# Splitting the last scaling and the residual add of an MoE block between VectorE and GpSimd

## The reference

```
y = routed + shared                     # 512 x 1024, the sum over the 8 experts of each token and the shared one
x = x + ga2 * rmsnorm(y, g_post_ffn)    # rmsnorm(y, g) = y * rsqrt(mean(y*y) + 1e-6) * g, mean over the 1024 channels
```

## Time and profile before

| | us |
|---|---|
| median of 3 runs | 1064.5 (1063.95 to 1066.36) |
| profiled execution, its own time | 1069.23 |
| its span in the trace | 1067.2 |
| granted TensorE clock, mean over the span | 0.981 |
| busy: TensorE / VectorE / ScalarE / GpSimd | 1020.3 / 872.1 / 645.2 / 295.4 |

### The profile page before, as it was taken

The page is one execution under the profiler, slowest core; times in us unless marked ns, Lnnn a source line. Parts: engine busy times, 40 slices in busy tenths (PEclk is TensorE's granted clock), DMA queues, the critical chain, the costliest instruction groups (busy, mean ns, idle before and its releaser), DMA issues.

```text
span 1067.2 us, 15239 instructions
## 1 busy us (share of the span) xinstructions
PE 1020.3 (96%) x4652; PEld 742.9 (70%) x4652; DVE 872.1 (82%) x1416; ACT 645.2 (60%) x743; POOL 295.4 (28%) x224
## 2 busy tenths in 40 slices
PE   4999999899998999999999999999999999999976
PEld 0687776567754777777777777777777777777732
DVE  1669877734768899999999889999989999999867
ACT  5334135733343678777777767777767777777511
POOL 1242231630302433223323213323313323332200
PEclk9899999989999999999999999999999999999997
DMA  9667752212254799999999999999999999999993
GB/s 338 263 223 280 267 179 97 69 30 90 99 217 146 284 376 373 364 381 379 393 386 381 360 367 359 377 376 385 369 364 345 364 343 328 353 354 362 361 413 152
DMA packets 71080, 318.67 MB, mean 299 GB/s; under 512 B 17232, under 2 KB 17744, under 8 KB 44560
## 3 DMA queue, kind: packets, MB, share of 16 engines
q1 hardware_dynamic: 36816, 200.30, 49.7%
q10 hardware_dynamic: 11616, 72.66, 17.9%
q0 software_dynamic: 22624, 45.40, 11.4%
HBM read 317.25 MB, written 39.85 MB: 335 GB/s over the span
## 4 chain that ended last, share of the span: by engine, by line
PE 80%; DVE 9%; DMA 7%; ACT 2%; issue 1%; ACTq 0%; SPq 0%; POOL 0%; DVEq 0%; POOLq 0%
PE ps L1348 11%; PE ps L1350 11%; PE ps L1349 11%; PE ps L1366 10%; PE ps L1033 8%; PE ps L1372 8%; PE ps L1123 6%; DMA hg<-h_rows,idxg 3%; PE ps L1225 2%; DMA yr<-y_rows 2%; PE ps L1285 2%; PE ps L1049 2%; PE ps L1305 1%; PE ps L1207 1%; DVE acc L1504 1%
## 5 line engine op out<-in xcount | busy, mean ns | idle before, releaser
L1821 DVE TENSOR_TENSOR wlo<-raw,whi 128x2048 fp32r<-128x2048 f32 x136 | 305.2, 2285 | 0.0
L891 ACT ACTIVATE whi<-raw 128x2048 fp32r<-128x2048 f32 x136 | 261.4, 1923 | 0.0
L1348 PE MATMUL ps<-whi,hthi 128*128 128x512 f32 x544 | 223.9, 412 | 0.0
L1350 PE MATMUL ps<-whi,htlo 128*128 128x512 f32 x544 | 213.5, 393 | 0.0
L1349 PE MATMUL ps<-wlo,hthi 128*128 128x512 f32 x544 | 212.7, 391 | 0.0
L661 POOL DMA_INDIRECT y_rows<-ysb,idxs x68 | 69.1, 1016 | 447.8 <-DVE idxg L1816 387.2
L934 ACT ACTIVATE ysb<-ps 128x1024 f32<-128x1024 f32 x68 | 69.8, 1026 | 176.1 <-PE ps L1372 176.1
L653 POOL DMA_INDIRECT hg<-h_rows,idxg x70 | 135.9, 1942 | 71.9 <-DVE idxg L1816 51.6
L1366 PE MATMUL ps<-rawd,actt 128*128 128x512 f32 x272 | 129.4, 598 | 1.9 <-ACT actt L927 1.9
L1350 PEld LDWEIGHTS ps<-whi,htlo 128*128 128x128 f32 x544 | 102.1, 188 | 22.3
L1349 PEld LDWEIGHTS ps<-wlo,hthi 128*128 128x128 f32 x544 | 102.6, 189 | 17.7
(11 more groups left out here) (273 smaller groups left out, 1608.7 us busy)
## 6 DMA issues: line engine op xcount, KB each, us to landing
raw<-in_w_gate_dram SPq DMA_DIRECT2D x68, 1024.0 KB
raw<-in_w_up_dram SPq DMA_DIRECT2D x68, 1024.0 KB
rawd<-in_w_down_dram ACTq DMA_DIRECT2D x66, 1024.0 KB, 10.1
ada<-in_w_ada_dram SPq DMA_DIRECT2D x24, 1024.0 KB, 7.8
yr<-y_rows SPq DMA_DIRECT2D x6, 2048.0 KB, 19.1
wraw<-in_w_in_dram POOLq DMA_DIRECT2D x8, 1024.0 KB, 5.6
woraw<-in_w_out_dram SPq DMA_DIRECT2D x16, 256.0 KB, 2.7
yr<-y_rows SPq DMA_DIRECT2D x8, 512.0 KB, 10.1
```

The lines of the kernel that those rows point to most:

```text
L891: A(whi[:, s, m_, :], raw[:, s, m_, :], ACT.Copy).then_inc(hi_ok, 1)
L1348: mm(out_, hthi[s][:, k, :], hi, start=(k == 0), stop=False)
L1350: ins = mm(out_, htlo[s][:, k, :], hi, start=False, stop=(k == KD - 1))
L1821: V.tensor_tensor(wlo[s][:, m_, :], raw[:, s, m_, :], whi[:, s, m_, :].bitcast(F32), ALU.subtract).then_inc(lo_dve, 1)
```

## The change

VectorE's `rows_done(t)` no longer calls `weighted` between `var` and the root. After the factor is ready it makes one operation over 1024 columns: the sums from TensorE's banks, times the factor of the row, times `ga2`, into `yr[0]`. For row blocks 0, 1 and 2 this raises a new semaphore `branch_ok`, and GpSimd adds `yr[0]` to the residual `xs` in two halves of 512 columns, each raising `out_ok`. For row block 3 VectorE waits for its own operation and adds the two halves itself, each raising the new `out_last`, on which SyncE waits for the last two writes. The five small operations of the factor, the order on VectorE, the sums of TensorE and the squares of ScalarE stay as they are.

```diff
         out_ok = sem("out_ok")
+        out_last = sem("out_last")
+        branch_ok = sem("branch_ok")
...
             for t in range(TT):
                 for hf in range(2):
                     cols = slice(hf * 512, (hf + 1) * 512)
-                    sp.wait_ge(out_ok, 2 * t + hf + 1)
+                    if t < TT - 1:
+                        sp.wait_ge(out_ok, 2 * t + hf + 1)
+                    else:
+                        sp.wait_ge(out_last, hf + 1)
                     sp.dma_start(out[t * P:(t + 1) * P, cols], xs[:, t, cols]).then_inc(out_done, 16)
...
             scatter(m + (E // 2 - 1), 1)
+            for t in range(TT - 1):
+                gp.wait_ge(branch_ok, t + 1)
+                for hf in range(2):
+                    cols = slice(hf * 512, (hf + 1) * 512)
+                    gp.tensor_tensor(xs[:, t, cols], xs[:, t, cols], yr[0][:, t, cols], ALU.add).then_inc(out_ok, 1)
...
-            def weighted(t):
-
-                v.wait_ge(ypart_mm, t + 1)
-                return V.tensor_tensor(yr[0][:, t, :], bank(Y_BANK[t], 2), ga2[:, :], ALU.mult)
-
             def rows_done(t):
 
-                factor(ST_S, D, t, t + 1, between=lambda: weighted(t))
+                factor(ST_S, D, t, t + 1)
+                ins = V.scalar_tensor_tensor(out=yr[0][:, t, :], in0=bank(Y_BANK[t], 2), scalar=rs[:, ST_S, t:t + 1],
+                                             in1=ga2[:, :], op0=ALU.mult, op1=ALU.mult)
+                if t < TT - 1:
+                    ins.then_inc(branch_ok, 1)
+                    return
+                then(ins)
                 for hf in range(2):
                     cols = slice(hf * 512, (hf + 1) * 512)
-                    V.scalar_tensor_tensor(out=xs[:, t, cols], in0=yr[0][:, t, cols], scalar=rs[:, ST_S, t:t + 1],
-                                           in1=xs[:, t, cols], op0=ALU.mult, op1=ALU.add).then_inc(out_ok, 1)
+                    V.tensor_tensor(xs[:, t, cols], xs[:, t, cols], yr[0][:, t, cols], ALU.add).then_inc(out_last, 1)
```

## The result

| | before | after |
|---|---|---|
| median of 20 runs, us | 1066.17 (1063.95 to 1069.99) | 1069.88 (1065.86 to 1074.41) |
| ratio, 95% interval | | 1.0031 (1.0020 to 1.0042) |
| profiled execution / its span | 1069.23 / 1067.2 | 1071.64 / 1069.7 |
| start of the squares of block 0, in the trace | 1047.88 | 1048.20 |
| end of VectorE's last instruction | 64.69 | 67.18 |

(Times of the tail are given without the thousand from here on.) The change makes the kernel slower, by 0.2% to 0.4% in this timing (the two medians differ by 3.71 us). With 17 more runs of the kernel before, its own median is 1.67 us higher than the 1064.5 of the first three. The tail is 2.17 us longer; 1.95 were forecast.

The account below looks back on a forecast made before the run. VectorE bounds the tail, TensorE's sums next; two GpSimd waits turn a block's 2.60 into 4.22 against 3.61, moving the end from 64.69 to 66.64. That +1.95 on 1064.5 gives about 1066.4 us, range 1063.0 to 1067.6.

Parts of the forecast that it names:

- no change: Whole kernel: a measured difference within 0.2%, 2.1 us, either way; given 64%.
- What bounds the kernel: Tail: VectorE is the limit, 1.58 us late for block 3's `var`; TensorE's sums come next.
- The open root and the fused operation: Tail on VectorE: uncovered root 0.43, new operation 1.28, next instruction 1.20 behind its start, block 3's first addition 1.32.
- The small operations wait: Tail: two-tensor column operations wait for GpSimd's halves, two waits worth 1.6 a block, making it 4.22; 47%.
- the second rival: Tail: one wait a block, not two, only L1487 waiting; +0.92 us, 1065.4; 12%.
- the slower rival: Tail: operations with one SBUF input, the reciprocal too, also wait; 4.42 a block, +2.75 us, 1067.2; 14%.
- The cast that spoke for that rival: Earlier trace: a VectorE cast from SBUF took 2.36 where 0.42 is usual, cited as a sign of waiting.
- The two semaphores at nothing: Outside the tail's work: the two new semaphores were taken to add no time.
- the one from the sum to the time: Whole kernel: the profiled execution's 4.73 above the median carries over, so 1064.5 + 1.95 gives about 1066.4.
- slower by over 0.2%: Whole kernel: the outcome of slowing by more than 0.2%, given 32% together.
- the 2.13 that I called the bound: Whole kernel: the slowdown in us over which the forecast counted the change as slower, against its 1.95.

Follow-up runs that it names:

- e1: Kernel after, with the tail's three two-tensor column operations taking the second operand as a scalar per row; tail 15.76 us, ratio 1.0008.
- e12: Kernel after, with a shorter factor using scalars per row and block 3 in the form of before; tail 15.07 us, ratio 0.9978.
- e2: Kernel after without GpSimd's additions, VectorE adding the halves of all four blocks; tail 18.02 us, ratio 1.0011.
- e5: Kernel before with the two new semaphores declared and not used; tail 16.82 us, ratio 1.0022.
- e11: The same kernel as e5, timed once more; tail 16.83 us, ratio 0.9990.
- e15: The same kernel as e1, timed once more; tail 15.55 us, ratio 0.9981.

## Why the prediction was wrong, by its own steps

The forecast said no change, on its slower edge, 1066.4 us in a range to 1067.6; the measured median is 1069.88. The difference of 3.5 us has three parts: 1.67 is the base (1064.5 of three runs, 1066.17 of twenty), 0.2 the tail, and about 1.6 is in this timing alone and not in the tail; what made it stays open, and the scatter of the repeated timings is large enough for it.

- **What bounds the kernel: right.** Before, VectorE was late by 1.6 for block 3, and TensorE came next. In e1 and e12 ScalarE's squares release `var` of block 3 and the gain stops there. (The forecast writes 3.43 for a block on TensorE and works with 3.46; the trace of before has 3.52 once and then 3.44 and 3.43 between the starts of the squares.)
- **The open root and the fused operation: right.** 0.42 from `var` to the reciprocal (0.43), 1.28 for the operation with 1.20 to the next (the same), 1.32 to the first addition (1.32). e2 adds them up to +1.21, where its expectation had +1.3.
- **The small operations wait: right, with its sizes.** L1494 0.61, 0.83 and 0.83, L1495 1.19 each; over blocks 1 to 3 the means are 0.76 and 1.19, where about 0.7 and 1.1 were forecast. A block is 4.27 where 4.22 were worked out, since GpSimd starts 0.16 behind `var` and not 0.12 (block 1 4.07 for 4.01). The tail was missed by 0.22: 0.06 ahead of block 1's `var`, 0.06 and 0.05 in blocks 1 and 2, 0.05 behind block 3's `var`. (Two figures of the forecast do not follow from its own steps: by 1.25 GpSimd's second half would end at 55.20, not 55.15, and block 1's new operation in the second rival comes at 55.20, not 55.29. Neither moves an end by more than 0.1.) That the waiting second half of GpSimd goes ahead of L1495 held in every block from 1 on. In e1 operations with one tensor input ran at 0.21 beside GpSimd. The rule that the forecast cited from the Trainium skill, SBUF — State Buffer, "Who interferes with whom", parts VectorE's instructions in this way, two SBUF inputs against at most one outside the two-port modes, and the traces agree on both sides: 1.19 for L1495, 0.16 for the reciprocal. I gave 14% to the slower rival, in which the reciprocal waits; it took 0.16. The cast that spoke for that rival had one SBUF input too and did wait (2.36 for 0.42, until 0.28 behind GpSimd's end); no run here was made to find out why it did and the column operations did not.
- **The two semaphores at nothing: right** as far as the runs go: between VectorE's end and the end of the span 2.51 before and 2.52 after, outside the span 2.03 before and 1.94 after, and the timings of e5 and e11 lie on both sides of 1.
- **The step that failed is the one from the sum to the time.** I took the difference of 4.73 between the profiled execution and the median of three runs as fixed, added 1.95 to a base of three runs that themselves lay 2.4 us apart (1063.95 to 1066.36), wrote that all before 1048 us was untouched, and put the range's upper end 1.2 us above the forecast, for the waits alone. The start of the tail moves by 6.0 us between two executions of one kernel, and even the median of twenty runs stands 1.67 from that of three. With that scatter the forecast of +1.95 had to carry a chance of "slower by over 0.2%" of about one half, and the range had to reach to 1070. The tail is now measured at +2.1 to +2.2, right on the 2.13 that I called the bound. So the mechanism was right; "no change" stood or fell with 0.2 us in the tail, and the range left no room for the scatter of the stages ahead of it.

## What to carry to other kernels

Handing VectorE's additions to GpSimd frees VectorE only if what VectorE does meanwhile does not wait for GpSimd. Here the column operations with two SBUF tensor inputs waited whenever GpSimd was adding: 0.16 us of work took up to 1.19, and 1.98 beside a GpSimd instruction of 1024 columns. So check the tiny operations too. One SBUF tensor input was free in the column operations and beside a PSUM input, but not in the cast of the earlier trace rows, so look at the durations in each case. Where a column operation has a second operand with one value per partition, give it as a scalar per row: that cost 0.05 us and took L1494 and L1495 from 0.83 and 1.19 to 0.21. And before an operation that covers a round trip to another engine is fused elsewhere, count what it covers: with all work on VectorE the fused form cost 0.3 us a block, and in the last block, which is VectorE's alone, the form of before takes 3.68 from `var` to the end (e12) where the fused one takes 4.16 (e1 and e15); the shorter factor is 0.03 of that at most.

## What the runs showed that had not been expected

- The waits show up as busy time of VectorE, and the chain of waits names no releaser for them. The sign is a duration many times that of the same line elsewhere: L1495 takes 0.16 at its least and 1.19 at its most in one trace.
- A scalar per row lengthens an operation of one column from 0.16 to 0.21, two of them to 0.27, so merging two operations in this way saved 0.02 to 0.03 a block and not 0.19.
- One GpSimd instruction of 1024 columns (2.34) cost VectorE more than two of 512 (2.48 together), 4.41 a block against 4.27.
- The stages ahead of the first gather vary by 6.5 us between executions of one kernel (it starts at 326.1 and at 332.6), three times what this change moves.
